# Redistributing VectorE work between the columns of an expert-activation stage: late picks, late gate units and a new deal of dot products

## The reference, cut to what matters

```python
q = (xb @ wq).reshape(PEER_BLOCK, PEER_HEADS, 2, PEER_HALF)
s = jnp.einsum('thpd,hpkd->thpk', q, subkeys)            # 8 heads, 2 x 128 keys
s_top, i_top = lax.top_k(s, PEER_TOPK)                   # 16 of 128, twice
cand = s_top[:, :, 0, :, None] + s_top[:, :, 1, None, :] # 16 x 16 candidates
cand_idx = i_top[:, :, 0, :, None] * PEER_KEYS + i_top[:, :, 1, None, :]
g_s, g_i = lax.top_k(cand, PEER_TOPK)                    # 16 of 256
e = jnp.take_along_axis(cand_idx, g_i, axis=-1)          # expert numbers
g = jax.nn.softmax(g_s, axis=-1)
act = jax.nn.gelu(jnp.einsum('thed,td->the', u[e], xb))  # u: 16384 experts x 1024
return jnp.einsum('the,thed->td', g * act, v[e])
```

## Time and profile before

| | us |
|---|---|
| median of three runs | 2231.81 |
| lowest and highest run | 2225.08, 2232.66 |
| profiled execution, its own time | 2228.25 |
| its span, first to last instruction | 2226.6 |
| TensorE busy in the span | 2030.9 |
| VectorE busy in the span | 1604.2 |
| stage of the change, first to last column matmul | 975.1 to 1667.4 |

### The profile page before, as it was taken

The page is one execution under the profiler, slowest core; times in us unless marked ns, Lnnn a source line. Parts: engine busy times, 40 slices in busy tenths (PEclk is TensorE's granted clock), DMA queues, the critical chain, the costliest instruction groups (busy, mean ns, idle before and its releaser), DMA issues.

```text
span 2226.6 us, 32324 instructions
## 1 busy us (share of the span) xinstructions
PE 2030.9 (91%) x10471; PEld 1637.8 (74%) x10471; DVE 1604.2 (72%) x3110; ACT 854.5 (38%) x1715; POOL 579.9 (26%) x599
## 2 busy tenths in 40 slices
PE   8998999669879999969899799979998999999997
PEld 7774576234446558869899789979997888888885
DVE  3563256775224346889999899989758999999988
ACT  1232022113202221124676476647853333333331
POOL 1000133332200000001222223223325555554540
PEclk9999899878989999989999899999999999999998
DMA  5333232997850231437799699969989999999992
GB/s 199 80 74 116 85 100 71 328 358 265 295 228 3 114 105 57 130 105 235 246 315 304 231 295 323 307 227 330 369 313 395 394 403 392 396 389 397 383 391 94
DMA packets 239937, 547.81 MB, mean 246 GB/s; under 512 B 22190, under 2 KB 122335, under 8 KB 238394
## 3 DMA queue, kind: packets, MB, share of 16 engines
q1 hardware_dynamic: 110714, 287.40, 36.7%
q0 software_dynamic: 60736, 208.40, 25.5%
q10 hardware_dynamic: 68352, 50.34, 6.9%
HBM read 485.58 MB, written 60.02 MB: 245 GB/s over the span
## 4 chain that ended last, share of the span: by engine, by line
PE 34%; DVE 18%; issue 6%; ACT 3%; DMA 2%; ACTq 0%; SPq 0%; DVEq 0%; POOLq 0%
PE psum L2805 22%; PE psum L2559 7%; DVE u_gather L2457 4%; PE psum L2116 3%; DVE hT L2485 2%; PE psum L2575 1%; DVE uL L2231 1%; DVE eq L2027 1%; ACT hT L2420 1%; DVE eq L2024 1%; DMA S<-activation_table 1%; DVE vecs L2028 1%; ACT uH L2363 1%; DVE cand L1989 1%; ACT hT L2415 1%
## 5 line engine op out<-in xcount | busy, mean ns | idle before, releaser
L2221 POOL DMA_INDIRECT u_gather<-in_u_rows,gather_ids x160 | 186.7, 1167 | 847.2 <-DVE dots L2457 497.2
L2559 PE MATMUL psum<-hH,uH 128*128 128x384 f32 x1024 | 354.3, 346 | 49.2 <-DVE uL L2231 49.2
L2559 PE MATMUL psum<-hH,uL 128*128 128x384 f32 x1024 | 346.4, 338 | 0.0
L2559 PE MATMUL psum<-hL,uH 128*128 128x384 f32 x1024 | 346.2, 338 | 0.0
L2805 PE MATMUL psum<-vH,wH 128*128 128x512 f32 x768 | 302.0, 393 | 11.3 <-DVE wL L2749 11.3
L2805 PE MATMUL psum<-vH,wL 128*128 128x512 f32 x768 | 300.9, 392 | 0.0
L2667 POOL DMA_INDIRECT v_gather<-in_v_rows,idx_now x160 | 236.9, 1481 | 245.8 <-DVE y_sample L2756 146.6
L2805 PE MATMUL psum<-vL,wH 128*128 128x512 f32 x768 | 300.7, 392 | 0.0
L2559 PEld LDWEIGHTS psum<-hH,uH 128*128 128x128 f32 x1024 | 195.3, 191 | 52.8 <-DVE uL L2231 52.4
L2457 DVE CUSTOM_DVE_ANT_0 u_gather<-u_gather,h 128x1024 f32<-128x1024 f32 x160 | 195.4, 1221 | 4.0
L2559 PEld LDWEIGHTS psum<-hL,uH 128*128 128x128 f32 x1024 | 195.7, 191 | 0.0
(11 more groups left out here) (510 smaller groups left out, 3331.5 us busy)
## 6 DMA issues: line engine op xcount, KB each, us to landing
u_raw<-in_uT SPq DMA_DIRECT2D x128, 512.0 KB, 5.3
S<-in_v_rows SPq DMA_DIRECT2D x64, 512.0 KB, 11.0
v_rest<-in_v_rows SPq DMA_DIRECT2D x64, 512.0 KB, 6.7
activation_table<-acts ACTq DMA_DIRECT2D x128, 192.0 KB, 4.6
gate_table<-Gtile ACTq DMA_DIRECT2D x48, 512.0 KB, 7.0
S<-gate_table SPq DMA_DIRECT2D x16, 768.0 KB, 7.3
S<-activation_table SPq DMA_DIRECT2D x16, 768.0 KB, 13.4
G_rest<-gate_table SPq DMA_DIRECT2D x16, 768.0 KB, 8.2
```

The costliest lines, as they stand in the source:

```text
L2221: c.nc.gpsimd.indirect_dma_start(c.ug[:, k % RG], None, c.A["u_rows"].rearrange("j i d -> (j i) d"), bass.IndirectOffsetOnAxis(ap=c.ids[:, ...
L2559: ins = nc.tensor.matmul(column[n % 4][:, 0:ND], w[:, n % RU, d], x[:, d], start=m == 0, stop=m == len(parts) - 1)
```

## The change

The change alters the order within `steps`, and the tables, and leaves all computations as they are.

- The picks of heads 4 to 7 of a tile stood all in the last step of the phase that routes it, one behind the other in `route`. For tiles 2 and 3 they now stand in the first step of the next phase, one at each of its first four places (`late_picks`). Tile 1 is routed in phase 0 by a list of its own, and keeps its picks there.
- The first step of phases 1 to 3 now has nine columns in place of 5, 5 and 4. `tile_gates` moves from place 1 to place 3. The four units and the four pieces of routing of this step stood behind all its columns; now the pieces of routing stand at places 5 to 8, the one-hot rows (`hots`, which was a part of `unit` on VectorE) at places 6, 6, 7, 8, and the units of ScalarE and TensorE at places 6, 7, 8, 8.
- The other steps have fewer columns, so that each phase has as many columns as before.
- The dots: 9, 38, 43, 56 in the four phases and 14 in the tail, where there were 9, 47, 50, 48 and 6. Within a step they are spread evenly over the places.

```diff
-STEP_COLS = ((2, 1) * 4, (5, 5, 5, 5, 5, 5, 4, 4), (5,) * 8, (4, 3) * 4)
-STEP_DOTS = ((1, 1, 1, 0, 0, 2, 2, 2), (6,) * 7 + (5,), (7, 6, 6, 6) * 2, (6,) * 8)
-TAIL_DOTS = (2, 1, 1, 1, 1, 0)
+STEP_COLS = ((2, 1) * 4, (9, 4, 4, 4, 5, 4, 4, 4), (9, 5, 4, 4, 5, 4, 4, 5), (9, 3, 3, 2, 3, 3, 2, 3))
+STEP_DOTS = ((1, 1, 1, 0, 0, 2, 2, 2), (13, 4, 3, 3, 4, 4, 4, 3), (8,) + (5,) * 7, (7, 6, 7, 8, 7, 7, 8, 6))
+TAIL_DOTS = (3, 3, 3, 2, 2, 1)
...
-                    routed, gates = st == (0 if p else 5), st == (0 if p else 7)
+                    routed, gates, first = st == (0 if p else 5), st == (0 if p else 7), st == 0 and p > 0
+                    places = max(U_STEP, nc_)
...
-                    for i in range(max(U_STEP, nc_, nd)):
+                    for i in range(places):
                         if i < nc_:
                             columns(n)
                             n += 1
-                        if i < nd:
+                        for _ in range(i * nd // places, (i + 1) * nd // places):
                             dot(k)
                             k += 1
                         if routed and i == 0:
                             gates_out(p)
-                        if gates and i == 1:
+                        if first and i < U_STEP:
+                            late_picks(p, i)
+                        if gates and i == 3:
                             tile_gates(p)
-                        if st == 0 and i == 4 and p:
+                        if first and i == 4:
                             slots_in(p)
+                        if first and i >= 6:
+                            for m in range((0, 2, 3)[i - 6], (2, 3, 4)[i - 6]):
+                                hots(p, st, m)
+                            for m in range((0, 1, 2)[i - 6], (1, 2, 4)[i - 6]):
+                                unit(p, st, m)
+                        if first and i >= 5:
+                            route(p, st, i - 5)
                         if st and i < U_STEP:
                             if p:
+                                hots(p, st, i)
                                 unit(p, st, i)
                             route(p, st, i)
-                    if st == 0:
+                    if st == 0 and p == 0:
                         for i in range(U_STEP):
                             route(p, st, i)
-                        for i in range(U_STEP if p else 0):
-                            unit(p, st, i)
...
+                def late_picks(p, i):
+                    if p > 1:
+                        router.pick(BATCH + i, b.res)
...
                         elif st % BATCH == BATCH - 1:
                             router.convert(b.first, BATCH)
-                            if st == PH - 1:
-                                for h in range(BATCH, PH):
-                                    router.pick(h, b.res)
```

More of the change, by code:

```diff
@@ L2269, in gates_of, with steps @@
             return c.res0[:, 2] if p == 0 else b.res[:, 2] if p < STILE else c.resS[:, 2]
-        def steps(columns, dot, tile_pre, gates_out, tile_gates, slots_in, unit, route, flush):
+        def steps(columns, dot, tile_pre, gates_out, late_picks, tile_gates, slots_in, hots, unit, route, flush):
             n = k = 0
@@ L2336, in columns @@
                         sp.dma_start(u[:, n % RAW], A["uT"][n]).then_inc(u_in[n % RAW], 16)
-                steps(columns, *[nothing] * 8)
+                steps(columns, *[nothing] * 10)
                 sp.wait_ge(res_ready, STILE)
@@ L2438, in flush @@
                         store(NTB - 1, i)
-                steps(columns, nothing, nothing, gates_out, nothing, slots_in, unit, nothing, flush)
+                steps(columns, nothing, nothing, gates_out, nothing, nothing, slots_in, nothing, unit, nothing, flush)
             @block.vector
@@ L2475, in tile_gates, with hots @@
                                          ALU.mult), res_ready)
-                def unit(p, st, i):
+                def late_picks(p, i):
+                    if p > 1:
+                        router.pick(BATCH + i, b.res)
+                def hots(p, st, i):
                     n = unit_of(p, st, i)
@@ L2543, in columns @@
                     low_u(c, dve, n)
-                steps(columns, dot, tile_pre, nothing, tile_gates, nothing, unit, route, nothing)
+                steps(columns, dot, tile_pre, nothing, late_picks, tile_gates, nothing, hots, nothing, route, nothing)
                 dve.wait_ge(c.dot_done, NDOT)
@@ L2577, in unit @@
                     ins.then_inc(g_mm, 1)
-                steps(columns, nothing, nothing, nothing, nothing, slots_in, unit, nothing, nothing)
+                steps(columns, nothing, nothing, nothing, nothing, nothing, slots_in, nothing, unit, nothing, nothing)
 FINAL = (0, 1, STILE, 2, 3)
```

## The result

The changed kernel takes 2218.96 us (median of 9 runs, 2211.72 to 2224.48), the kernel before, beside it, 2231.81 us. The ratio is 0.9947, with a 95% interval of 0.9933 to 0.9961. So the change is worth about 12 us (12.9 between the medians) where 37 were forecast, and 2219 lies outside the range of 2177 to 2211. The profiled execution took 2221.12 us with a span of 2219.4.

A forecast was written before the change was run, and what follows sets the result against it. TensorE, busy 91%, was held to lose 73.2 us, mostly waiting for VectorE in phases 1 and 2. Remaining losses 5.2 + 1.5 + 12.4 + 5.1 + 12 = 36.2; gain 37 from 2228.25 gives 2191 us, range 2177 to 2211.

The forecast's parts named there:

- The bound and its price: Whole stage: TensorE loses 73.2 us in waits and lower clock, all but 3 where VectorE has no slack.
- the pace of 4.16 and 0.90: TensorE without waits: 4.16 us for a column and 0.90 us for a unit, used to price each window.
- Picks, dots and softmax: Phases 1 and 2: VectorE's load falls just under TensorE's, the softmax wait goes at no cost; 1.5 us of loss kept.
- The 9.32 ahead of column 54: End of phase 1: TensorE's 9.32 us wait behind four picks in a row on VectorE, forecast to go.
- the 5.78 of the softmax: Soon after those picks: VectorE stands still 5.78 us for ScalarE's Exp, forecast to go when `tile_gates` comes two places later.
- the rival of VectorE as the bound: Phases 1 and 2: half of their inner loss stays, 18.7 us for 1.5, ending at 2208 us; chance 0.08.
- Boundaries: First steps of phases 1 to 3: 12.4 us of new waits plus 5.1 of lower clock replace 9.2 lost at each.
- Phase 3 and the tail: From phase 3's second step on: the DMA needs 143 us at 385 GB/s, TensorE 131.1, VectorE 135.5.
- The "12" in the sum of losses: Loss in us from phase 3's second step to the tail's end: 143 of DMA time above TensorE's 131.1.
- my own last sentence: Sign of being wrong: over 20 us of uL waits before phase 3, or over 155 us from its second step to the last column.
- The rival at 373 GB/s: Phase 3 and tail: the DMA runs at 373 GB/s, the stretch takes 148 us, ending at 2196 us; chance 0.16.
- The gather rival: Phase 3 and tail: late gathers hold back VectorE's columns and TensorE; gain eaten at a 180 us stretch; chance 0.05.

The follow-up runs named there:

- e11: Changed kernel with a gate block's four 512 KB stores behind every second of eight units, not behind the first four; 2212.32 us, ratio 0.9913.
- e1: Changed kernel with the new order but the old number of dots per phase (9, 47, 50, 48, 6), spread evenly; 2219.58 us, ratio 0.9955.
- e14: Changed kernel with phase 3's old columns and old first-step order, late picks kept, seven dots a step, and gate stores spread; 2220.52 us, ratio 0.9953.
- e13: Changed kernel with gate stores spread behind every second unit and dots dealt 9, 42, 46, 52 and 11; 2205.88 us, ratio 0.9896.
- e15: Changed kernel with gate stores spread behind every second unit and dots dealt 9, 44, 48, 51 and 8; 2208.01 us, ratio 0.9888.
- e5: Changed kernel with six gather buffers instead of five; 2221.65 us, ratio 0.9956.
- e8: Changed kernel fetching 2 KB instead of 4 KB of each row from gather 97 on, the dot reading that half twice; 2197.9 us, ratio 0.9859.

## Why the prediction was wrong

*The bound and its price: right.* The sum of losses, the pace of 4.16 and 0.90, and VectorE as the cause in phases 1 and 2 hold. VectorE's busy time in the windows of phases 1 and 2 fell to 187.2 and 189.3 us (forecast 183.8 and 189.5, for slightly fewer columns).

*Picks, dots and softmax: right, with 2.8 us too little kept for loss.* The 9.32 ahead of column 54 and the 5.78 of the softmax are gone. Phases 1 and 2 lose 4.3 us for the 1.5 forecast; most of it is one wait of 2.01 us for uL ahead of column 92, at the end of phase 2, and the lower clock behind it (0.76 from 1438 to 1445 us). The margins were as thin as feared, but the rival of VectorE as the bound did not come.

*Boundaries: right in mechanism, a little dear.* Behind the seventh column TensorE waits for the first gates, as this row of phase 2 has it:

```profile
1276.70 2.07 PE L2585 MATMUL psum<-hT 128*128 128x128 f32 x8 [4.16 <-ACT hT L2429]
```

I had 4.2. The next window shows the lower clock behind it:

```profile
1278.40:1284.10 5.70, 5.70 (x26) 5.70 (x26) 5.53 (x14) 3.08 (x8) 1.87 (x2) 0.72 0.94 293
```

The three boundaries cost 20.3 us for 17.5.

*Phase 3 and the tail: the step that failed.* The "12" in the sum of losses should have been 27.9. The bytes were right: 59.4 MB less 4.2 is 55.2, and 56.0 were moved. The rate was wrong, and with it the idea that bytes by a rate give the time. I took 385 GB/s from a mean of 373 and the best 20 us before, and the stretch ran at 357, in 157.0 us for 143. That is 14.0 of the 15.9 us; the other 1.9 are a slip in the sum, which took the tail at its measured 26.9 us as if nothing were lost in it, where six columns at the pace need 25.0. By my own last sentence (over 155 us) this was the mark of being wrong. The rival at 373 GB/s had the right sign but not the size. The DMA can do more: e11 moves the same bytes at 383. And bytes by a rate don't tell the time: for the 48.6 MB of e1 my sum has no loss at all, and e1 lost 22.5 us. I read the DMA as one pipe with a rate, and not as queues that share it and can hold the engine that starts a store. What the runs showed in its place is ScalarE held in such starts, and TensorE waiting 18.8 us for its gates. A row of the kernel before shows what I passed over, at 1550.42:

```profile
1550.42 4.01 ACTq L2373 DMA_DIRECT2D activation_table<-acts  x1
1554.48 0.60 ACT L2392 ACTIVATE Gtile<-psum 128x512 f32<-128x512 f32 x1 [4.09 <-issue]
```

With five columns taken away from the rest of the phase and 16 dots added, such holds came four times, 24.3 us in all. Of the 15.9 us above the forecast, the spacing of the stores alone gives back 9.6 (e11). VectorE was never the longer one in this stretch: it was busy for 123.1 us, where I had 135.5.

The Trainium skill, "DMA: Bandwidth & Descriptors", in "Where 436 GB/s comes from", has about 358 GB/s for transfers between HBM and SBUF, and by it, as an estimate, the stretch would have been 154 us. That comes close to the 157 measured at a mean of 357. Yet the trace does not bear the rule out as a ceiling: e11 holds 383 over 147 us and, in this window, 405:

```profile
1560.00:1580.00 20.00, 20.00 (x133) 19.95 (x132) 16.93 (x24) 15.31 (x38) 10.78 (x9) 1.00 1.05 405
```

*What had no term.* The gathers of the tail delay the first loads of the expert stage: 3.2 us in the gap and 3.4 in the experts, where TensorE waits that much longer for wL. e1, with the old number of dots in the tail, has neither. I priced the tail by VectorE, TensorE and the bytes up to the last column, and asked of no transfer what comes behind it.

So the forecast of 37.0 goes to the 7.1 between the two profiled executions: 15.9 in phase 3 and tail, 6.6 behind the stage, 2.8 at boundaries, 2.8 within phases 1 and 2, 0.2 at the start, and 1.9 of the stage's later begin, 30.2 in all (rounded). The medians, with 12.9 us, are kinder than this one pair of profiles. The gather rival was far off: dots waited for gathers only 8.7 us in all.

## What to carry to other kernels

When work moves into a stretch whose DMA share is already 1, don't price it by its bytes and a mean rate alone: look for the starts of transfers that took long before, as the 4.01 us here, and for what the engine that makes them does for others. Here it was the queue with packets of 570 bytes beside gathers of 3.6 KB. Spacing such stores out gave back 9.6 us in the changed order, but it takes from the time that a buffer has until it is written again, and in e14 that cost more than it brought. A tail of a stage is also the head of the next one, so give a transfer moved there a price behind the stage too.

The best version of the lot keeps the new order, spreads the stores and deals the dots about half way back: 2205.88 and 2208.01 us (e13, e15), 25 us under the kernel before each on its chip and twice what the change brought.

## What the hardware showed that I had not expected

- A start of a DMA by ScalarE or SP mostly takes 0.33 to 0.45 us, but in the changed kernel up to 7.9 us, and 13.9 with a sixth gather buffer (e5), and nothing behind it on that engine runs meanwhile. At the four long ones of the changed kernel 0.6 to 1.1 MB stood in the queue by the estimate above.
- While 3.6 KB gather packets and 570 byte store packets compete, the stores get 96 of 397 GB/s (1.06 of 4.37 MB in 11 us).
- Equal bytes, 56 MB, went through in 147.4 and in 157.0 us, with nothing changed but the spacing of the stores. With 48.6 MB and the stores in a bunch it was 151.8 us (e1).
- Halving the bytes of 63 gathers was worth some 20 us (e8), more than any reordering.
